# A memory branch's values multiplied at the start of a fused two-block kernel, with the opening's loads and the late conditioning chunks in another order

## The reference

```python
cond = silu(c) @ ada_w + ada_b              # shift1, scale1, gate1, shift2, scale2, gate2
h = rmsnorm(x, norm1_g) * (1 + scale1) + shift1
u, v, val, gate = split(h @ w_in + b_in)    # 512 columns each
y_a = gelu(u) * (causal_w @ layernorm(gelu(v)) + b_s)
y_b = silu(groupnorm(depthwise_conv31(val * sigmoid(gate))))
x = x + gate1 * (concat(rmsnorm(y_a), rmsnorm(y_b)) @ w_out)
...                                         # feed-forward, final norm, second block's mixer
m = rmsnorm_2(mem_2, mem_norm_2)            # 256 memory rows
kv = m @ xattn_wkv_2                        # 512 columns of keys, 512 of values
k, v = rmsnorm_2(kv[keys], k_norm), kv[values]
```

## Time and profile before

| | |
|---|---|
| three runs, us | 762.83, 768.16, 761.18 |
| median, us | 762.83 |
| profiled execution, span from first to last instruction, us | 769.1 |
| PE busy | 709.7 us, 92% |
| DVE busy | 361.4 us, 47% |
| ACT busy | 325.2 us, 42% |
| DMA | 211.44 MB, mean 275 GB/s |

### The profile page before, as it was taken

How to read it: one execution, slowest core, us unless ns; L and a number is a source line. 1 busy time by engine, 2 the same in 40 slices (tenths; PEclk the granted TensorE clock), 3 DMA queues, 4 the chain that set the end, 5 groups by cost and what they waited for, 6 DMA issues and landing times.

```text
span 769.1 us, 13134 instructions
## 1 busy us (share of the span) xinstructions
PE 709.7 (92%) x5455; PEld 561.9 (73%) x5456; DVE 361.4 (47%) x718; ACT 325.2 (42%) x690; POOL 61.2 (8%) x72
## 2 busy tenths in 40 slices
PE   4889999999999999999999999997999999879786
PEld 2685768887999999999988777876875555344352
DVE  2459967447545555444579589444431111111011
ACT  2365734726444443334566895857321111001011
POOL 0400002000000002000000028162000000000000
PEclk9899999989999999999898999999989999989997
DMA  9998979409667644455453346568869999999996
GB/s 335 354 404 336 370 290 334 157 23 375 218 238 240 222 164 166 169 176 164 164 198 132 124 141 196 164 219 356 308 271 422 421 421 419 420 421 419 421 408 216
DMA packets 75683, 211.44 MB, mean 275 GB/s; under 512 B 7463, under 2 KB 34245, under 8 KB 61798
## 3 DMA queue, kind: packets, MB, share of 16 engines
q1 hardware_dynamic: 74578, 209.91, 72.4%
q0 software_dynamic: 800, 0.63, 0.5%
q10 hardware_dynamic: 244, 0.03, 0.0%
HBM read 209.51 MB, written 1.05 MB: 274 GB/s over the span
## 4 chain that ended last, share of the span: by engine, by line
PE 65%; DMA 13%; DVE 10%; ACT 6%; SPq 3%; issue 2%; ACTq 0%; DVEq 0%
PE ps L1974 10%; PE ps L1975 9%; PE ps L1976 9%; PE ps L2699 6%; PE ps L1987 4%; PE ps L1988 4%; PE ps L1989 4%; DMA ring<-in_expert_w_up_dram 4%; DMA ring<-in_expert_w_gate_dram 4%; DVE YT L1341 3%; DVE ring_low L1225 3%; DMA Z<-in_expert_w_up_dram 3%; SPq L457 3%; PE ps L2668 3%; PE ps L2741 3%; DMA ring<-in_w_in_dram 2%
## 5 line engine op out<-in xcount | busy, mean ns | idle before, releaser
L1225 DVE TENSOR_TENSOR ring_low<-ring,HI 128x1024 fp32r<-128x1024 f32 (+1 forms) x119 | 142.0, 1236 | 27.0 <-ACT HI L712 26.9
L712 ACT ACTIVATE HI<-ring 128x1024 fp32r<-128x1024 f32 (+1 forms) x135 | 133.5, 1055 | 29.0 <-DMA ring<-in_w_in_dram 29.0
L1974 PE MATMUL ps<-AH,HI 128*128 128x256 f32 x320 | 90.1, 282 | 0.3 <-DVE Z L1492 0.3
L1976 PE MATMUL ps<-AH,ring_low 128*128 128x256 f32 x320 | 89.6, 280 | 0.0
L1975 PE MATMUL ps<-AL,HI 128*128 128x256 f32 x320 | 89.5, 280 | 0.0
L2699 PE MATMUL ps<-ring,ZM 128*32 128x256 f32 x880 | 72.7, 421 | 13.7 <-DMA ring<-in_expert_w_up_dram 10.7
L1974 PE MATMUL ps<-HI,AH 128*128 128x512 f32 (+1 forms) x176 | 71.7, 407 | 2.0 <-DVE ring_low L1225 1.0
L1975 PE MATMUL ps<-ring_low,AH 128*128 128x512 f32 (+1 forms) x176 | 69.1, 392 | 0.0
L2699 PEld LDWEIGHTS ps<-ring,ZM 128*32 128x32 f32 x880 | 34.6, 120 | 41.2 <-DMA ring<-in_expert_w_up_dram 14.1
L1987 PE MATMUL ps<-AH,HI 128*128 128x256 f32 x192 | 57.7, 301 | 7.3 <-DVE AL L1311 5.7
L1976 PE MATMUL ps<-HI,AL 128*128 128x512 f32 (+1 forms) x160 | 62.6, 391 | 0.0
(11 more groups left out here) (394 smaller groups left out, 1293.6 us busy)
## 6 DMA issues: line engine op xcount, KB each, us to landing
ring<-in_expert_w_up_dram SPq DMA_DIRECT2D x28, 1024.0 KB, 24.7
ring<-in_expert_w_gate_dram SPq DMA_DIRECT2D x27, 1024.0 KB, 26.2
ring<-in_expert_w_down_dram SPq DMA_DIRECT2D x24, 1024.0 KB, 23.9
ring<-in_w_ffn_in_dram SPq DMA_DIRECT2D x20, 1024.0 KB, 6.5
ring<-in_w_in_dram SPq DMA_DIRECT2D x18, 1024.0 KB, 6.0
ring<-in_ada_w_dram SPq DMA_DIRECT2D x16, 1024.0 KB, 9.1
ring<-in_w_ffn_out_dram SPq DMA_DIRECT2D x11, 1024.0 KB, 7.1
ring<-in_ada_w_dram SPq DMA_DIRECT2D x16, 512.0 KB, 11.1
```

The lines of the kernel that those rows point to most:

```text
L712: act(HI[:, (i + 1) % UNITS, 0:w], W.view(name)[:, o:o + w], ACT.Copy).then_inc(s_hi, 1)
L1225: tt(W.low(name)[:, o:o + w], W.view(name)[:, o:o + w], HI[:, (i + 1) % UNITS, 0:w].bitcast(F32), ALU.subtract).then_inc(s_lo, 1)
L1974: mm(dst, lh, rh, start=start, stop=False)
L1976: return mm(dst, ll, rh, start=False, stop=stop)
```

## The change

The memory's rows and the values' weights go to the front. SP loads `mem_2`, `kv_v0`, `x`, `kv_v1` in this order and only then the conditioning and `in_v0`. The gain `mem_norm_2` gets a row tile of its own (`rowsm`), transposed first. PE transposes the raw memory rows first of all, ACT and DVE write `MH` and `ML` from them with the gain alone, and the root of the mean square is applied after the product, as a scale by row, where ACT copies the values (`VM`) and later the keys (`KS`) out of PSUM. Between the units of the values' strip PE transposes `x` and takes the first conditioning load. The rows of POOL are issued once `s_ada` is 8, not 4; the spatial weights `wsv` are loaded behind `in_u0`, not before `in_v1`, and are transposed one half at a time in the `in_u` strip (`spatial_turned`), both halves through one bank, so that ACT has a copy to make between two `hi_to` calls. `ada(2, *)` leaves the `in_w` strip and stands behind the mixing, among the small products of the norms, where the values' strip stood. `columns_half(1)` moves into the second unit of `in_g0`. The third condition's copy (`condition(3, 7)`) follows the group norm.

```diff
 def split_order():
-    out = [f"{w}{h}" for h in "01" for w in ("in_v", "in_g")] + [f"{w}{h}" for w in ("in_u", "in_w", "kv_v") for h in "01"]
+    out = ["kv_v0", "kv_v1"] + [f"{w}{h}" for h in "01" for w in ("in_v", "in_g")] + [f"{w}{h}" for w in ("in_u", "in_w") for h in "01"]
@@ SP @@
+            for t in range(NT):
+                const(MX[t], A["mem_2"].rearrange("o (t p) d -> p (o t) d", p=P)[:, t, :], s_mem)
+            W.apart("ada", 4)
+            rows128("kv_v0", w_kv, 512, 512, 0, 4)
             const(X[:, :, :], A["x"].rearrange("o (t p) d -> p (o t) d", p=P), s_x)
+            rows128("kv_v1", w_kv, 512, 512, 4, 4)
             ada_half(0, range(4))
...
+            sp.wait_ge(s_mn, 4)
+            const(wsv, A["a_spatial_w"].rearrange("o h t s -> t (o h) s"), s_ws)
             ada(A["ada_w"], 1, (0, 1), 2048)
             rows128("in_u1", w_in, 512, 512, 4, 4)
-            sp.wait_ge(s_rp, 3)
-            for t in range(NT):
-                const(MX[t], A["mem_2"].rearrange("o (t p) d -> p (o t) d", p=P)[:, t, :], s_mem)
             ada(A["ada_w"], 1, (2, 3), 2048)
...
-            rows128("kv_v0", w_kv, 512, 512, 0, 4)
+            for h in range(2):
+                rows128(f"out{h}", w_out, 0, D, 2 * h, 2)
             ada(A["ada_w"], 2, (0, 1, 2, 3), 4096)
-            rows128("kv_v1", w_kv, 512, 512, 4, 4)
-            ada(A["ada_w"], 2, (4, 5), 4096)
-            rows128("out0", w_out, 0, D, 0, 2)
-            ada(A["ada_w"], 2, (6, 7), 4096)
-            W.together([7, 0, 1, 2, 3, 4, 5, 6])
-            for h in range(1, 4):
+            for h in range(2, 4):
                 rows128(f"out{h}", w_out, 0, D, 2 * h, 2)
+            ada(A["ada_w"], 2, (4, 5, 6, 7), 4096)
+            W.together([0, 1, 2, 3, 6, 7, 4, 5])
@@ POOL @@
-            po.wait_ge(s_ada, 4)
+            po.wait_ge(s_ada, 8)
+            po.wait_ge(s_mtp, 4)
+            po.wait_ge(s_mn, 4)
@@ ACT @@
             upper_half(0)
-            hi_to(3)
+            ac.wait_ge(s_mn, 7)
+            ac.wait_ge(s_un, S.end["kv_v1"])
+            for t in range(NT):
+                act(VM[:, t, :], ps[(5, 6)[t]][:, :], ACT.Copy, scale=mst[:, 4 + t:5 + t]).then_inc(s_vm, 1)
+            hi_to(iv + 3)
...
+            def spatial_turned(hh):
+                ac.wait_ge(s_wtp, hh + 1)
+                act(WT[:, 4 * hh:4 * hh + 4, :], ps[6][:, :].rearrange("p (h s) -> p h s", h=4), ACT.Copy).then_inc(s_wt, 1)
...
             diagonals(0)
+            spatial_turned(0)
             hi_to(iu + 1 + AHEAD)
...
+            spatial_turned(1)
             hi_to(iu + 2 + AHEAD)
@@ DVE @@
                     if k0 == 0:
-                        lo_to(0)
+                        lo_to(iv)
+                    if k0 == 6:
+                        lo_to(iv + 4)
@@ PE @@
+            te.wait_ge(s_mem, 32)
             for kk in range(4):
                 for k in (2 * kk, 2 * kk + 1):
                     for t in range(NT):
-                        ins = tr(ps[kk][:, 256 * (k % 2) + P * t:256 * (k % 2) + P * t + P], X[:, t, by128(k)], ident[:, :])
-                ins.then_inc(s_xp, 1)
+                        ins = tr(ps[MTB[kk]][:, 256 * (k % 2) + P * t:256 * (k % 2) + P * t + P], MX[t][:, by128(k)], ident[:, :])
+                ins.then_inc(s_mtp, 1)
...
+            strip(("kv_v0", "kv_v1"), (5, 6), 0, 0, None, between_memory, MH, ML, low=s_ml)
...
+                if i < 2:
+                    spatial_turned(i)
+                if i == 2:
+                    spatial_sums()
...
-                for k in ((), (0, 1), (2, 3, 4), (5, 6, 7))[i]:
-                    ada(2, k)
```

More of the change, by code:

```diff
@@ L756, in _, with memory_upper @@
             ac.wait_ge(s_set, MATS)
-            ac.wait_ge(s_c0, 16)
+            ac.wait_ge(s_c0, 32)
             act(ccol[:, :], ccol[:, :], ACT.Silu).then_inc(s_cr, 1)
             warm(ACT.Sqrt)
+            iv = S.first["in_v0"]
+            def memory_upper(kk):
+                ac.wait_ge(s_mtp, kk + 1)
+                for k in (2 * kk, 2 * kk + 1):
+                    ins = act(MH[:, k, :], ps[MTB[kk]][:, 256 * (k % 2):256 * (k % 2) + 256], ACT.Copy, scale=gain_m[:, k:k + 1])
+                ins.then_inc(s_mh, 1)
+            ac.wait_ge(s_rc, 1)
+            for kk in range(2):
+                memory_upper(kk)
+            hi_to(0)
+            for kk in range(2, 4):
+                memory_upper(kk)
+            hi_to(3)
             ac.wait_ge(s_x, 16)
@@ L765, in _ @@
             act(RTS[0], RTS[0], ACT.Sqrt, scale=1.0 / D, bias=eps[:, 0:1]).then_inc(s_rn, 1)
+            for t in range(NT):
+                for n in range(2):
+                    if t or n:
+                        ac.wait_ge(s_mn, 2 * t + n)
+                    act(JM, MX[t][:, 512 * n:512 * n + 512], ACT.Square, scale=1.0 / 32,
+                        accum_out=mst[:, 2 * t + n:2 * t + n + 1]).then_inc(s_mn, 1)
+            ac.wait_ge(s_mn, 5)
+            act(mst[:, 4:6], mst[:, 4:6], ACT.Sqrt, bias=eps[:, 0:1]).then_inc(s_mn, 1)
             def upper_half(h):
-                hi_to((0, 5)[h])
+                if h == 0:
+                    hi_to(iv)
                 ac.wait_ge(s_m, h + 1)
@@ L871, in _ @@
                 act(AH[:, k, :], YA[:, k, :], ACT.Copy).then_inc(s_ah, 1)
-            hi_to(ik + 3 + AHEAD)
-            for h in range(2):
-                ac.wait_ge(s_gn, h + 1)
-                act(GQ[:, 2 * h:2 * h + 2, :], CV[:, 2 * h:2 * h + 2, :], ACT.Square).then_inc(s_sqs, 1)
-            hi_to(io + AHEAD)
             rooted(RGS, ps[3][:, 0:16], SUM_G)
             warm(ACT.Silu)
-            ac.wait_ge(s_un, S.end["kv_v1"])
-            for t in range(NT):
-                act(VM[:, t, :], ps[(2, 6)[t]][:, :], ACT.Copy).then_inc(s_vm, 1)
-            for i in (1, 2, 3):
-                hi_to(io + i + AHEAD)
+            hi_to(io + 6)
             for h in range(2):
@@ L1269, in _, with memory_lower @@
             copy(cr[:, :, :], bc(ccol[:, :], 2, [P, 8, 32])).then_inc(s_cr, 1)
+            iv = S.first["in_v0"]
+            ve.wait_ge(s_rp, 1)
+            copy(gain_m, ps[4][:, 64:72]).then_inc(s_rc, 1)
+            def memory_lower(kk):
+                ve.wait_ge(s_mh, kk + 1)
+                for k in (2 * kk, 2 * kk + 1):
+                    ins = stt(ML[:, k, :], ps[MTB[kk]][:, 256 * (k % 2):256 * (k % 2) + 256], gain_m[:, k:k + 1],
+                              MH[:, k, :].bitcast(F32), ALU.mult, ALU.subtract)
+                ins.then_inc(s_ml, 1)
+            ve.wait_ge(s_rc, 1)
+            for kk in range(2):
+                memory_lower(kk)
+            lo_to(0)
+            for kk in range(2, 4):
+                memory_lower(kk)
+            lo_to(3)
             for kk in range(4):
@@ L1386, in _ @@
             taps(22, 26)
-            for kk in range(4):
-                ve.wait_ge(s_mh, kk + 1)
-                for k in (2 * kk, 2 * kk + 1):
-                    ins = stt(ML[:, k, :], ps[MTB[kk]][:, 256 * (k % 2):256 * (k % 2) + 256], C1[:, NM + k:NM + k + 1],
-                              MH[:, k, :].bitcast(F32), ALU.mult, ALU.subtract)
-                ins.then_inc(s_ml, 1)
             lo_to(iw + 3 + AHEAD)
-            taps(26, 30)
-            condition(3, 7)
-            ik, io = S.first["kv_v0"], S.first["out0"]
-            lo_to(ik + AHEAD)
+            taps(26, TAPS)
+            io = S.first["out0"]
             for ct in range(4):
@@ L1407, in _ @@
                 tt(YA[:, 2 * h:2 * h + 2, :], YA[:, 2 * h:2 * h + 2, :], U[:, 2 * h:2 * h + 2, :], ALU.mult).then_inc(s_my, 1)
-            taps(30, TAPS)
-            lo_to(ik + 1 + AHEAD)
+            for h in range(2):
+                ve.wait_ge(s_gmp, h + 1)
+                tt(CV[:, 2 * h:2 * h + 2, :], CV[:, 2 * h:2 * h + 2, :], tiles(ps[(3, 6)[h]][:, :], 2), ALU.subtract).then_inc(s_gn, 1)
+            lo_to(io + 3)
             def rows_scaled(y, c, gain, r, i):
@@ L2116, in _, with by_channel @@
             columns_half(0)
[L2118 removed]
+            def by_channel(names, place, n, starts, between, q0=0, inside=None):
                 us = [u for x in names for u in range(S.first[x], S.end[x])]
```

271 lines of the change are left out of this document (124 added, 147 removed).

## The result

The changed kernel takes **776.92 us** (median of 4 runs, 775.99 to 782.57), the kernel before 762.55 (4 runs, 761.18 to 768.16). Its time is 1.0188 times that of before, 95% interval 1.0143 to 1.0233. A second comparison on another chip gave 775.40 (6 runs, 772.55 to 781.30) against 766.18, ratio 1.0132 (1.0077 to 1.0186). The forecast was 759.8 in a range of 751 to 767, so it missed by 17 us and on the other side of before. The ratios leave out the slowest executions (those more than 1.5% above their kernel's fastest); the medians and means given here are over every timed run. The ten runs of the changed kernel average 776.9, the 109 of before in all groups 766.7.

A forecast was written before the change was run, and what follows sets the result against it. It took the front as bound by bytes, the middle by PE or what feeds it, the end by bytes. Opening +6.9 and middle -9.4 gave -2.5, rounded to -3: 759.8 us from the median 762.8, range 751 to 767.

The forecast's parts named there:

- What lies behind the projection is unchanged: Feed-forward, mixer and experts: unchanged but for scales riding on copies that ACT makes anyway.
- Part 3: The opening, to the end of the gate's strip: PE becomes the bound, G = 63.3, +6.9 us.
- rival B: Early values' strip at 1.2 GHz, 0.20 us per slow matmul: 769 for all 48, 763 for about 16; chance 0.13.
- a bound of 4.7: Opening: +4.7 us more if half of the 48 early matmuls run at 1.2 GHz.
- rule and row: Clock at `in_v0`: full rate after dense work, or half rate after an idle chain, opening then 1.4 us longer.
- The late lower half: Opening: the lower half of `in_v1` stands behind two pairs of activation halves, there at 51.7, 1.9 us late.
- The loads: Opening: 2.5 MB more, net, ahead of `in_v1`; by bytes alone it lands at 44.4, +3.5 us.
- Parts 1 and 2: The middle, from the gate's strip to the projection's fifth row: work leaving and coming in, -9.4 us together.
- The columns' wait: PE at the second condition's columns: DVE copies 4.0 us later, the wait grows from 0.9 to 3.6, +2.7 us.
- The wait for a load: Behind the mixing: the last four conditioning loads need slots the first four free only there, +0.9 us.
- rival D: Late conditioning loads arrive one after another, 2.7 us each; four cost 7 us instead of 0.9: 766; chance 0.08.
- Rival C: The middle's PE saving is lost to DVE's later taps, leaving the norms' chains bare: 762; chance 0.12.

The follow-up runs named there:

- its variants: The changed kernel with idle transposes, the third condition partly back, the opening reordered, or several of these; 79 runs, lowest 763.35 us.
- The thinned strip: The kernel before with 8 of the 48 matmuls of the memory values' strip, in its old place; ratio 0.9995 (0.9938 to 1.0052).

## Why the prediction was wrong

The forecast's sum was +6.9 for the opening, -9.4 for the middle, nothing behind it. Measured against the second profile of before, in the changed kernel's first and second profile:

| step | forecast | first | second |
|---|---|---|---|
| opening, to the end of the gate's strip | +6.9 | +10.3 | +9.2 |
| from there to the fifth row (before 99.4) | -9.4 | -2.6 | -8.7 |
| behind the fifth row | 0 | +6.1 | +11.8 |
| sum | -2.5 | +13.8 | +12.3 |

**"What lies behind the projection is unchanged" was the step that failed**, and with it the carrying over of the difference to the median: 6 of the 16 us between forecast and first profile, 12 of the 15 in the second. The instructions there are unchanged; their time isn't, since falls of the granted clock at 380 to 424 and at 530 to 572 us come in some executions and not in others. Before takes 603.1 us behind the fifth row without them and 613.3 with them, the changed kernel 609.2 and 614.9 in its two profiles, and by the times of its ten runs it never went without. Why the changed kernel and its variants lose there in every run isn't settled: none of their 89 runs is under 763.3 us, though several have their fifth row as early as before or earlier. A delay in the kernel before shows that its later part can lose some 5 us more than the delay itself; that it is the position that does it in the changed kernel isn't shown.

**The sum was made from the one kind of execution and taken off the other.** The first profile of before had those falls itself (clock low in slices 20 and 22 of the earlier trace rows). Against its 769.1 us span I expected 766.1; the changed kernel's spans are 774.5 and 773.0, a miss of 8.4 and 6.9, of which at most 1.6 us lie behind the fifth row. But the same 3 us were taken off a median of 762.8, which by its time belongs to the executions without the falls, and that made the miss 17. A second profile would have shown that the same instructions vary by 8 us, and that my 1% for what can be told was too narrow for the range.

**Part 3 was mis-sized by 2.3 to 3.3 us**, and by more in its own places: the gate's strip ended at 68.4 and 67.4, not 63.3, while before's second profile has its end at 58.2 and not at 56.4, mostly by a fall in `in_v1`. The strip's first product came 0.7 to 0.9 us later than 12.1. Some 12 of its products in the first profile and 8 in the second ran at 1.2 GHz, so its first two units took 8.2 and 7.4 us, not 5.5: rival B, to a quarter of the strip and inside the limit of 16 that I gave it. My value had nothing for it; half of the strip stood beside it as a bound of 4.7. I had read the clock as full until 16 us, and that reading was wrong: the 16 transposes of `x` in the earlier trace rows took 3.27 us, and 16 such took 1.91 in the changed kernel behind dense work; the record shows 1.00 for both. For `in_v0` both cases came, behind the same waits of 0.8 and 2.8 us: in the first profile at full rate (so I took the rule of the Trainium skill, TensorE: Matmul & The Clock Gate, Part 1: The HAM clock gate), in the second at half rate from 37.3 to 40.7, 1.5 us longer, after nine products at full rate. So these traces don't decide between rule and row. And the first profile paid the same 1.5 us later, in `in_v1`, for which I had nothing. The late lower half, 2.2 us, was as forecast at 1.9. The loads were priced too low, 3.5 us for 2.5 MB where my own 2.7 us for each MB gives 6.8, without effect: ACT waited 0.7 us for `w_in`. What I had right is that PE's chain bounds the changed opening: shortening it on PE alone brought the first `in_v0` product 1.9 to 3.1 us forward.

**Parts 1 and 2 were right in their sum where the clock held, and partly by luck.** 90.7 and 90.9 us against 90.1. The columns' wait is 3.17 (forecast 3.6). But DVE waited for ACT's split only once, 1.44 us, where I had 2.2 and 1.8, and its copy came 2.0 to 2.4 us later behind the gate's strip, not 4.0; PE, counted from the gate's end, reached the columns as early as before, and not 1.3 us later. So the columns cost 2.0 to 2.4 us, where my terms gave 4.0. The wait for a load took that back: 3.00 to 3.27, not 0.9. That is rival D in small, and the wait goes when the first four chunks are used early. And in the first profile the clock fell in the new thin places between 103 and 111 and between 134 and 149 us: 6.2 us more than in the second, where the bound for it was 2.

**Rival C** said the gain would vanish by DVE; it was wrong in its cause. The thinned strip shows that half of its thought was right: the strip in its old place was cover, work that fills the waits between two chains of ACT and DVE. The changed kernel puts conditioning chunks in its place there.

## What to carry to other kernels

Moving dense work out of a busy stretch into the opening pays only what the opening can hide: 11 us of strip cost 9 to 10 there, 4 to 5 of them its products and 5.4 the loads, transposes and splits that came with it. When a step goes ahead of a chain, look at every in-order engine, not at the one that computes: the same reorder of the opening brought the next strip 1.9 to 3.1 us forward or 2.6 us back, by where VectorE's two instructions stood. Take two or three profiles of the kernel before; where the same instructions differ by several us between them, the range of any forecast has to hold that spread, also behind the last instruction that the change touches.

## What the runs showed of the hardware

The granted clock's record can read full while products run at half rate: 0.43 us from start to start between 13.0 and 18.3 us in the first profile of the changed kernel, 0.23 later, with 1.00 in the window of both.

```profile
13.00:18.30 5.30, 5.27 (x12) 4.13 (x13) 4.95 (x7) 5.20 (x8) 0.00 (x0) 1.00 1.05 387
23.00:30.00 7.00, 7.00 (x43) 5.09 (x43) 1.39 (x5) 0.00 (x0) 0.00 (x0) 1.00 0.82 279
```

The clock also falls while PE is busy throughout: 10.00 of 10.00 us at 0.66 from 380 to 390 in the second profile, behind 32 sums of one column each from 379 to 383. The same sums in before's second profile brought no fall. A delay of 1.7 us of dense work cost 7.2 on the mean of 12 runs, uncertain by 2. In the experts' stretch falls cost nothing: it took 202.5 to 202.8 us in four profiles whose falls there differ.
